# The second layer norm of a two-layer decoder step: its sums taken along the down-projection on a shifted residual, part of the centring on GpSimd, the output stored in four parts

## The reference, cut to what matters

```python
x = _layer_norm(ALPHA * x + mixed, ln1_w, ln1_b)
ff = jnp.square(jax.nn.relu(x @ w_up)) @ w_down
x = _layer_norm(ALPHA * x + ff, ln2_w, ln2_b)

def _layer_norm(x, w, b):
    mu = jnp.mean(xf, -1, keepdims=True)
    var = jnp.mean(jnp.square(xf - mu), -1, keepdims=True)
    return (xf - mu) * lax.rsqrt(var + EPS) * w + b
```

## Time and profile before

| | us |
|---|---|
| median of three runs (834.85 to 836.22) | 835.95 |
| the profiled execution's device time | 836.35 |
| its span in the trace | 834.6 |
| mean granted TensorE clock in it | 0.948 of full |

### The profile page before, as it was taken

The page is one execution under the profiler, slowest core; times in us unless marked ns, Lnnn a source line. Parts: engine busy times, 40 slices in busy tenths (PEclk is TensorE's granted clock), DMA queues, the critical chain, the costliest instruction groups (busy, mean ns, idle before and its releaser), DMA issues. The chain is left out here.

```text
span 834.6 us, 18462 instructions
## 1 busy us (share of the span) xinstructions
PE 749.3 (90%) x7662; PEld 711.0 (85%) x7662; DVE 577.6 (69%) x1056; ACT 416.0 (50%) x760; POOL 36.0 (4%) x44
## 2 busy tenths in 40 slices
PE   4779678988999999989997989799899999999994
PEld 4669667788999999989986988587799999999993
DVE  7997995445778899885445789834577886666443
ACT  4726131444577755446345624444466874455323
POOL 4000010210000000000010002010000000000000
PEclk9989886998999999999996999899899999999998
DMA  8442111352435455444441333413144555555521
GB/s 330 150 143 85 53 53 50 114 203 74 141 123 179 167 177 192 159 145 142 173 152 51 102 104 105 143 51 110 55 173 139 184 172 187 178 177 178 179 99 53
DMA packets 30580, 113.61 MB, mean 136 GB/s; under 512 B 3521, under 2 KB 3729, under 8 KB 29985
## 3 DMA queue, kind: packets, MB, share of 16 engines
q1 hardware_dynamic: 27936, 101.83, 36.6%
q0 software_dynamic: 1984, 9.52, 3.0%
q10 hardware_dynamic: 576, 1.08, 0.3%
HBM read 108.24 MB, written 4.18 MB: 135 GB/s over the span
## 5 line engine op out<-in xcount | busy, mean ns | idle before, releaser
L1436 DVE TENSOR_TENSOR w_low<-w_raw,w_high 128x1024 fp32r<-128x1024 f32 x192 | 236.5, 1232 | 152.3 <-ACT w_high L1014 149.6
L1014 ACT ACTIVATE w_high<-w_raw 128x1024 fp32r<-128x1024 f32 x192 | 202.5, 1055 | 242.6 <-PE stream L963 231.5
L961 PE MATMUL stream<-a_high,w_high 128*128 128x264 f32 x768 | 237.9, 310 | 33.7 <-DVE a_low L1441 21.7
L962 PE MATMUL stream<-a_low,w_high 128*128 128x264 f32 x768 | 229.2, 298 | 0.0
L963 PE MATMUL stream<-a_high,w_low 128*128 128x264 f32 x768 | 228.4, 297 | 0.0
L961 PEld LDWEIGHTS stream<-a_high,w_high 128*128 128x128 f32 x768 | 155.8, 203 | 44.3 <-issue 22.4
L962 PEld LDWEIGHTS stream<-a_low,w_high 128*128 128x128 f32 x768 | 156.3, 204 | 0.3
L963 PEld LDWEIGHTS stream<-a_high,w_low 128*128 128x128 f32 x768 | 155.7, 203 | 0.0
L961 PE MATMUL stream<-h_high,w_high 128*128 128x264 f32 x512 | 148.6, 290 | 1.2 <-issue 0.5
L962 PE MATMUL stream<-h_low,w_high 128*128 128x264 f32 x512 | 145.1, 283 | 0.0
L963 PE MATMUL stream<-h_high,w_low 128*128 128x264 f32 x512 | 145.0, 283 | 0.0
(11 more groups left out here) (369 smaller groups left out, 953.7 us busy)
## 6 DMA issues: line engine op xcount, KB each, us to landing
w_raw<-in_weights SPq DMA_DIRECT2D x192, 512.0 KB, 3.3
mats<-in_matrices POOLq DMA_DIRECT2D x2, 1024.0 KB, 5.5
S_hg<-in_state_hg POOLq DMA_DIRECT2D x2, 768.0 KB, 5.0
out_hg_s<-S_hg POOLq DMA_DIRECT2D x2, 768.0 KB, 3.7
consts<-in_constants POOLq DMA_DIRECT2D x1, 1484.5 KB, 9.2
X<-in_xT ACTq DMA_DIRECT2D x4, 264.0 KB, 5.7
out_y<-X SPq DMA_DIRECT2D x1, 1056.0 KB, 3.9
S_rt<-in_state_rt POOLq DMA_DIRECT2D x2, 512.0 KB, 7.1
```

The costliest lines, as they stand in the source:

```text
L961: pe.matmul(bnk[:, 0:width], wh, xh, start=(first and kk == 0), stop=False)
L962: pe.matmul(bnk[:, 0:width], wh, xl, start=False, stop=False)
L1014: act.activation(w_high[:, n % SPLIT_SLOTS, :], w_raw[:, n % RAW_SLOTS, :], ACT.Copy).then_inc(high_ready, 1)
L1436: put(tt(w_low[:, n % SPLIT_SLOTS, :], w_raw[:, n % RAW_SLOTS, :], w_high[:, n % SPLIT_SLOTS, :].bitcast(F32), ALU.subtract), low_ready)
```

## The change

The mean and the mean of squares are now both summed while the down-projection runs.

- After tiles 0 and 1 of the residual are complete (k = 5), PE sums them (ln2_shift). ACT scales by KT/2 and copies to ln1_shift: the mean over these two tiles. DVE subtracts this shift from tiles 0 to 3 at k = 7 and from 4 to 7 at k = 9, before or after the projection is added.
- ACT squares each shifted tile into X1 (ln2_square). PE sums the shifted tiles 2 to 7 (ln2_mu; those of tiles 0 and 1 sum to zero) and the squares of all eight (ln2_sq).
- Behind the last chunk, ACT copies the mean d to ln1_d and squares it, DVE takes the variance as mean of squares less d squared, ACT the root, DVE the reciprocal. d itself is subtracted by DVE from tiles 0 to 2 and by POOL from tiles 3 to 7 (centre, BY_POOL = 3).
- One DVE operation now multiplies a tile by the weight and the reciprocal. ACT adds the bias, in layer 0 straight into a_high. DVE makes a_low as (X + bias) - a_high. X itself gets its bias in layer 1 (ln2_output), two tiles in each of chunks 1 to 4.
- y is stored in four transfers of two tiles.

POOL's memset for layer 1 (L502 before) now stands behind its five subtractions. SP's four stores are the last on its queue, behind all weight loads.

```diff
-for _k in range(KT - 2):
-    _plan(DOWN_B + 2 * _k + 3, ("ln_mu_part", _k))
+_plan(DOWN_B + 5, ("ln2_shift", 0), ("ln2_shift", 1))
+_plan(DOWN_B + 9, ("ln2_mu", 2), ("ln2_sq", 0), ("ln2_sq", 1), ("ln2_sq", 2))
+for _k in range(3, KT - 1):
+    _plan(DOWN_B + 2 * _k + 3, ("ln2_mu", _k))
+    _plan(min(DOWN_B + 2 * _k + 5, N_CHUNKS - 1), ("ln2_sq", _k))
+_plan(N_CHUNKS - 1, ("ln2_mu", KT - 1), ("ln2_sq", KT - 1))
...
-_plan(N_CHUNKS - 1, ("ln2_mu",), ("ln2_var",))
...
+BY_POOL = 3
...
-            sp.wait_ge(ln_ready, 8 * DEPTH)
-            sp.dma_start(y_out, X[:, :, :]).then_inc(outs["y"], 16)
-            sp.wait_ge(outs["y"], 16)
+            for m in range(0, KT, 2):
+                sp.wait_ge(y_ready, m + 2)
+                sp.dma_start(y_out[:, m:m + 2, :], X[:, m:m + 2, :]).then_inc(outs["y"], 16)
+            sp.wait_ge(outs["y"], 16 * KT // 2)
...
+                def centre():
+                    pool.wait_ge(mean2_copied, l + 1)
+                    for m in range(BY_POOL, KT):
+                        pool.wait_ge(xc2_ready, 8 * l + m + 1)
+                        pool.tensor_tensor(X[:, m, :], X[:, m, :], ln1_d, ALU.subtract).then_inc(pool_centred, 1)
...
+                centre()
...
-            def ln_mu_part(l, u):
-
-                k = u[1]
-                b = unit(l, ("ln2_mu",)) if k == 0 else bank(l, ("ln2_mu",))
-                pe.wait_ge(res_ready, 8 * l + k + 1)
-                pe.matmul(b[:, 0:T], cv("model_mean"), X[:, k, :], start=(k == 0), stop=False)
-
-            def model_mean(l, u, ready, src):
-                mean = ready is res_ready
-                b = bank(l, u) if mean else unit(l, u)
-                for k in range(KT - 2 if mean else 0, KT):
-                    pe.wait_ge(ready, 8 * l + k + 1)
-                    mm = pe.matmul(b[:, 0:T], cv("model_mean"), src[:, k, :], start=(k == 0), stop=(k == KT - 1))
-                mm.then_inc(unit_done, 1)
...
+            def ln2_shift(l, u):
+                partial_mean(l, u, raw2_ready, 3 * l + u[1] + 1, X, 0, 1)
+
             def ln2_mu(l, u):
-                model_mean(l, u, res_ready, X)
-
-            def ln2_var(l, u):
-                model_mean(l, u, lnsq_ready, sq)
+                partial_mean(l, u, xc2_ready, 8 * l + u[1] + 1, X, 2, KT - 1)
+
+            def ln2_sq(l, u):
+                partial_mean(l, u, xsq2_ready, 8 * l + u[1] + 1, X1, 0, KT - 1)
...
+            def ln2_square(l, m):
+
+                act.wait_ge(xc2_ready, 8 * l + m + 1)
+                act.activation(X1[:, m, :], X[:, m, :], ACT.Square).then_inc(xsq2_ready, 1)
+
+            def ln2_step(l, c):
+
+                k = c - DOWN_B
+                if k == 6:
+                    b, fu = got(l, ("ln2_shift",))
+                    act.activation(ln1_shift, b[:, 0:T], ACT.Copy, scale=float(KT / 2)).then_inc(shift2_ready, 1)
+                    copied(shift2_ready, l + 1, fu)
+                if k == 8:
+                    for m in range(3):
+                        ln2_square(l, m)
+                elif k > 8 and k % 2:
+                    ln2_square(l, (k - 3) // 2)
+
             def norm(l):
+                ln2_square(l, KT - 1)
+                b, fu = got(l, ("ln2_mu",))
+                act.activation(ln1_d, b[:, 0:T], ACT.Copy).then_inc(mean2_copied, 1)
+                copied(mean2_copied, l + 1, fu)
+                act.activation(sq0, ln1_d, ACT.Square).then_inc(mean2_ready, 1)
+                act.wait_ge(var2_ready, l + 1)
+                act.activation(sq0, sq_r, ACT.Sqrt, bias=cv("eps")).then_inc(deviation2_ready, 1)
                 for m in range(KT):
-                    act.wait_ge(lnc_ready, 8 * l + m + 1)
-                    act.activation(sq[:, m, :], X[:, m, :], ACT.Square).then_inc(lnsq_ready, 1)
-                b, fu = got(l, ("ln2_var",))
-                act.activation(sq[:, 0, :], b[:, 0:T], ACT.Sqrt, bias=cv("eps")).then_inc(lnsd_ready, 1)
-                copied(lnsd_ready, l + 1, fu)
-
-                for m in range(KT):
-                    n = 8 * l + m + 1
-                    act.wait_ge(lns_ready, n)
-                    act.activation(X[:, m, :], sq[:, m, :] if m else sq0, ACT.Identity, scale=pv(l, "ln2_w")[:, m:m + 1],
-                                   bias=pv(l, "ln2_b")[:, m:m + 1]).then_inc(ln_ready, 1)
-                    if l < DEPTH - 1:
-                        act.wait_ge(ln_ready, n)
-                        act.activation(a_high[:, m, :], X[:, m, :], ACT.Copy).then_inc(ahigh_ready, 1)
+                    act.wait_ge(scaled2_ready, 8 * l + m + 1)
+                    to, done = (a_high, ahigh_ready) if l + 1 < DEPTH else (X, y_ready)
+                    act.activation(to[:, m, :], X[:, m, :], ACT.Identity, bias=pv(l, "ln2_b")[:, m:m + 1]).then_inc(done, 1)
+
+            def ln2_output(l, m):
+
+                act.wait_ge(a_ready, 24 * (l + 1) + m + 1)
+                act.activation(X[:, m, :], X[:, m, :], ACT.Identity, bias=pv(l, "ln2_b")[:, m:m + 1]).then_inc(x2_ready, 1)
...
+                        if l and c in (1, 2, 3, 4):
+                            ln2_output(l - 1, 2 * c - 2)
+                            ln2_output(l - 1, 2 * c - 1)
...
+                    if c > DOWN_B:
+                        ln2_step(l, c)
...
+                if l and m == 0:
+                    dve.wait_ge(x2_ready, 8 * l)
...
-                put(tt(X[:, m, :], X[:, m, :], p, ALU.add), res_ready)
+                put(tt(X[:, m, :], X[:, m, :], p, ALU.add), raw2_ready if m < 3 else xc2_ready)
                 free(fr)
+
+            def ln2_shifted(l, m, s=None):
+                put(tt(X[:, m, :], X[:, m, :], ln1_shift, ALU.subtract), s)
+
+            def ln2_step(l, c):
+
+                k = c - DOWN_B
+                if k % 2 == 0:
+                    residual_down(l, k // 2 - 1)
+                if k == 7:
+                    dve.wait_ge(shift2_ready, l + 1)
+                    for m in range(3):
+                        ln2_shifted(l, m, xc2_ready)
+                    ln2_shifted(l, 3)
+                    settle()
+                if k == 9:
+                    for m in range(4, KT):
+                        ln2_shifted(l, m)
+                    settle()
...
-                b, fu = got(l, ("ln2_mu",))
-                for m in range(KT):
-                    put(tt(X[:, m, :], X[:, m, :], b[:, 0:T], ALU.subtract), lnc_ready)
-                free(fu)
-                dve.wait_ge(lnsd_ready, l + 1)
-                chain(dve.reciprocal(sq_r, sq[:, 0, :]))
+                def centred(m):
+                    put(tt(X[:, m, :], X[:, m, :], ln1_d, ALU.subtract))
+
+                dve.wait_ge(mean2_copied, l + 1)
+                centred(0)
+                ms, fs = got(l, ("ln2_sq",))
+                dve.wait_ge(mean2_ready, l + 1)
+                put(tt(sq_r, ms[:, 0:T], sq0, ALU.subtract), var2_ready)
+                free(fs)
+                for m in range(1, BY_POOL):
+                    centred(m)
+                dve.wait_ge(deviation2_ready, l + 1)
+                chain(dve.reciprocal(sq_r, sq0))
+
                 def scaled(m):
-                    put(tt(sq[:, m, :] if m else sq0, X[:, m, :], sq_r, ALU.mult), lns_ready)
+                    if m >= BY_POOL:
+                        dve.wait_ge(pool_centred, (KT - BY_POOL) * l + m - BY_POOL + 1)
+                    put(stt(X[:, m, :], X[:, m, :], pv(l, "ln2_w")[:, m:m + 1], sq_r, ALU.mult, ALU.mult), scaled2_ready)
 
                 scaled(0)
                 scaled(1)
...
                     if m + 2 < KT:
                         scaled(m + 2)
                     if l + 1 < DEPTH:
-                        split_a(l + 1, 0, m, X, m)
-                if l == DEPTH - 1:
-                    settle()
+                        dve.wait_ge(ahigh_ready, 24 * (l + 1) + m + 1)
+                        put(stt(a_low[:, m, :], X[:, m, :], pv(l, "ln2_b")[:, m:m + 1], a_high[:, m, :].bitcast(F32), ALU.add, ALU.subtract), a_ready)
```

30 lines of the change are left out of this document (19 added, 11 removed).

## The result

The kernel after takes 831.06 us, the median of 20 runs (829.67 to 835.97), against 837.34 us for the kernel before, also 20 runs beside it (834.85 to 840.76). The ratio is 0.9928, with a 95% interval of 0.9912 to 0.9943: 6 us less, where 2.1 less was forecast. The profiled execution took 833.16 us with a span of 831.2, against 836.35 and 834.6. So the pair of profiles shows 3.4 us of difference in span.

What follows compares the result with a forecast made beforehand. TensorE was taken to bound the down-projection, with serial norm tails behind each layer's last chunk; layer 1 -1.15, layer 0 -1.71 and the bias +0.74 gave -2.12 us, from a median of 835.95 to 833.8, range 831.6 to 836.4.

Steps and rivals of the forecast that it cites:

- the last store: End of layer 1: the last store of y, now 264 KB, lands in 3.0 us instead of 3.9, -0.9 us.
- the clock at the restart: Layer 0 into layer 1: the clock rises 4.7 us after TensorE is fed without gaps, costing as much as before.
- Sums in the stream: Down-projection: five sums per layer moved between chunks cost 0.45 us each on full TensorE, +2.25 us per layer.
- rival (d): Sums between chunks wait for their squares and TensorE stalls, 0 to 1 us per layer: up to 835.8; 0.18 with (b).
- Up to the reciprocal: Tail of both layers: the reciprocal starts at 821.9 instead of 823.83 on layer 1's old clock times, -1.93 us.
- Rival (a): Tail: POOL's operation is slow (1.08 us) and VectorE pays twice, +2.26 us per tail: 838.3; chance 0.14.
- Layer 0 to the restart: Layer 0's tail until TensorE restarts: -1.93 us up to the reciprocal and -0.27 from there to the first block.
- Layer 1 behind the reciprocal: Layer 1's tail, reciprocal to the end of ScalarE's eight operations: 5.83 us instead of 6.40, -0.57.
- The feed behind the restart: Layer 0 into layer 1: a_low steps of 0.82 instead of 0.95 us, gapless from the sixth block, -1.76 us.
- Rival (b): Restart: the clock rises at the same instant, so 7.1 us run at half speed: 835.0; chance 0.18 with (d).
- The bias in chunk 3: Layer 1's chunk 3: two bias operations delay the weight copy for chunk 6 and VectorE's S5 work, +0.74 us.
- Rival (c): Tail and layer 1's first chunks: the lock bites less and the bias is hidden: 832.2; chance 0.20.

Runs made afterwards that it cites:

- no_pool: The kernel after with all eight tiles centred by VectorE and none by GpSimd (BY_POOL = 8): 835.7 us mean, ratio 0.9984.
- pool6: The kernel after with six tiles centred by GpSimd and two by VectorE (BY_POOL = 2): 832.3 us mean over 8 runs, ratio 0.9946.
- b_fill: The kernel before plus nine unused sums on TensorE behind layer 0's last sum: 837.0 us mean, ratio 0.9994.

## Why the prediction was right or wrong

The direction was right, the size was not, and 831.06 lies just below the range's low end of 831.6. Two terms of the sum failed: the last store was put at -0.9 us and is worth -1.85, and the clock at the restart was put at the same cost as before and costs about 1 us less. A third was not in the sum at all: where the clock's falls in the mixers lie. The mean of one unchanged kernel moved by 2 us between timings, and the clock accounts for 1.5 of it. Step by step:

- **Sums in the stream, +2.25 per layer.** Right: +2.24 and +2.26, and no stall of TensorE, so rival (d) did not occur.
- **Up to the reciprocal, -1.93.** Right within 0.1. It starts 4.98 us after the first sum; 4.88 was forecast. GpSimd's operation takes 0.65 us when VectorE has none beside it, exactly the value that was taken; the five take 3.72 us because three of them also wait for VectorE (0.90, 0.84, 0.84). That the two engines take turns holds, to the point that each operation ends a fixed time after the other's, 0.29 us (VectorE) and 0.52 (GpSimd). What the sum had otherwise is that GpSimd's first operation starts beside VectorE's first centring and not behind it, and that the second centring starts later, behind the variance; the two nearly cancel. The estimate of 0.58 us from the Trainium skill's "GPSIMD Engine Reference", section "3.1 Elementwise — side-by-side cycle accounting", was lower, and the measured 0.65 decides. The exclusive lock of the Trainium skill's "SBUF — State Buffer", section "SBUF: two separate sides", agrees with these rows and with no_pool and pool6: 0.35 us per centring without GpSimd, 0.73 beside it, and a first scaling of 0.88 us instead of 0.49 when GpSimd is still at work. Rival (a), which needed about 0.85 us for GpSimd's operation, is refuted.
- **Layer 0 to the restart, -2.20 with the step behind the reciprocal.** Right: -2.14.
- **Layer 1 behind the reciprocal, -0.57.** Right: ScalarE's last operation ends 5.70 us after the reciprocal's start, forecast 5.83, so -0.70.
- **The last store, -0.9. Wrong, half the size.** I drew a line through two transfers of other sizes, one of them a weight load (3.3 us, the median of 192), and read 3.0 us for 264 KB. It landed in 2.1 us. Measured with one edit alone: -1.85. Between the stores of 264 and 1056 KB the landing grows by 1.8 us, 0.23 us for each 100 KB; my line had 0.11.
- **The feed behind the restart, -1.76, with the clock costing as much as before. Wrong in the clock's part.** With the clock held in both kernels the place is worth -1.83, so the blocks' steps were sized well. The clock was put at the same 4.7 us after the gapless feed. In the kernel after the feed has no gaps from the sixth block on (442.41 + 4.10 = 446.5) and the rise comes at about 448.5, 2 us later. Its cost fell from 1.3 to 2.1 us to 0.3 to 0.9. That is about 1 us more of gain. What sets the instant of the rise stays open: over the profiles of the kernel after it comes 4.9 or 6.1 us after the restart. Rival (b), a rise at the same instant, was more wrong still.
- **The bias in chunk 3, +0.74.** Right: 0.80 at the place, and 0.6 to 0.9 in the column to chunk 84.
- **The baseline and the rest.** Repeating columns -2.06, the boundary -1.83 and about -1.0 for its clock, the bias +0.8: -4.1 us, of which the forecast had 2.1. Three timings gave -6.0, -3.9 and -5.1. The remaining 1.9 us of the first timing (0.9 over all three) are not in any place that the change touches. The mixers of either layer vary by 4 to 5 us between executions of unchanged code, which is enough for it, and the mean clock of the first timing's runs was the highest of the three (0.9500). By the scatter of the runs alone, the mean difference over all three timings is uncertain by some 0.8 us (an estimate), nearly the 0.9 that is left. A share that belongs to the change, by its later or earlier arrival at layer 1's mixers, is not excluded: I have no way to fix the instants, and four profiles of each are too few. This stays open. I subtracted 2.1 from 835.95, the median of three runs, when twenty gave 837.34. That baseline was 1.4 us too low and hid part of the error: from 837.34 the same sum gives 835.2, which is 4.2 us above the result and not 2.7.
- **Rival (c)** gave 832.2, nearest to the result, by a mechanism that is refuted: the ports did collide and the bias was not hidden.

What it would have taken: a range for the store's landing between 2 and 3.9 us instead of a line, since no row showed a small store alone, and a range for the clock's cost at the restart between nothing and that of before. Both errors lay on the side of more gain, 0.95 and about 1.0 us. And a spread of 2 us for the instants of the clock, which one profile can't show but the three given runs, 1.4 us apart, hinted at.

## What to carry to other kernels

Cut the profiled executions at instants that occur in each of them, and compare piece by piece: here that resolves 0.03 to 0.05 us where the whole time resolves 1 to 2, and it says at once which pieces are the change's. Where a piece moves with the clock, compare only profiles that have spent the same time at the lower level in it; so the bias's 0.8 us could be seen in a column that varies by 4. Before calling a surplus the change's own, profile and time the unchanged kernels again, since an interval over runs of one timing does not cover what moves between timings. A last store is worth splitting when only its landing is left at the end, and where work is shared with GpSimd, VectorE's own part ahead of the critical operation is what to shorten, and GpSimd's last tile may reach a little into what follows: in pool6 that took back 0.4 of 0.8 us.

## What the runs showed of the hardware

- A store of 264 KB lands in 2.0 to 2.1 us behind three others of the same size; one of 1056 KB takes 3.9. The difference shows in full at the end of the span, 1.85 us.
- GpSimd subtracts two float32 tiles of 128x264 in 0.65 us. Where VectorE centres beside it the same operation takes 0.84 to 0.90 us, and ends 0.52 us after VectorE's.
- VectorE issues the same subtraction every 0.35 us in a row of seven and takes 0.43 for a single one. Begun behind GpSimd's it takes 0.65 or 0.88, and ends 0.29 us after GpSimd's. The reciprocal, with one input, took 1.79 to 1.80 us with or without GpSimd beside it.
- With unused sums through layer 0's norm TensorE kept its clock at the upper level in five of seven profiles (1.00 over 26 us, against 0.51 over 14 us without). In b_fill that removed 1.3 to 2.1 us from the stretch behind it, and yet the means were 837.0 and 837.2. Part of the clock did not come: the twelve runs of b_fill have a mean granted clock of 0.9499 and the 35 of the kernel before beside them 0.9473, that is some 4 us less at the lower level in a run, where the profiles of the kernel before have 10.2 to 13.7 us at the restart alone. Whether it was given back elsewhere or not held in every run, the one profile does not show.
- The same code took 384.8 to 390.2 us up to chunk 84 of layer 0 over all profiles. Five pairs of profiles whose granted clock fell at the same instants there agree to between 0.03 and 0.18 us.
